# Fp32r products in one PSUM half: the 512-column head matmul becomes two matmuls of 256 columns

## What is computed

```python
proj = h @ w_in                      # even layer: SSD mixer and conformer convolution; odd layer: gated convolution and sparse attention
...
return jnp.concatenate([y, u], axis=-1) @ w_out

def conv_ffn(h, w_up, conv_w, conv_b, w_down):
    u = causal_dwconv(h @ w_up, conv_w, conv_b)
    g, v = jnp.split(u, 2, axis=-1)
    return (jax.nn.silu(g) * v) @ w_down
```

## Time and profile before

| | |
|---|---|
| device time, median of 3 runs | 2856.93 us (2853.34 to 2862.99) |
| profiled execution, span from first to last instruction | 2860.4 us |
| mean granted TensorE clock in it | 0.965 of 2.4 GHz |
| instructions | 41198 |

### The profile page before, as it was taken

One profiled execution on the slowest core, in us unless ns is written; L12 is line 12 of the kernel. 1 busy time (PEld: TensorE's weight loads), 2 busy tenths in 40 slices (PEclk: granted clock), 3 DMA queues, 4 the chain that ended last, 5 costly groups with the idle time before them and its releaser, 6 DMA issues.

```text
span 2860.4 us, 41198 instructions
## 1 busy us (share of the span) xinstructions
PE 2704.1 (95%) x15154; PEld 2330.6 (81%) x15154; DVE 1980.1 (69%) x2783; ACT 1328.3 (46%) x1716; POOL 418.8 (15%) x441
## 2 busy tenths in 40 slices
PE   6987788799999999999999999889999999999999
PEld 5866675688888888888888888767888888888887
DVE  6499987866776577567755576685667756675675
ACT  3444434344563455345433454463346634553553
POOL 4079953321000000000210000000210000000003
PEclk8888899899999999999989999999999999999999
DMA  5444441255555555555655566403555555555554
GB/s 177 134 145 132 132 132 60 78 186 185 184 190 183 184 190 183 185 191 172 190 158 164 176 178 190 132 1 100 187 184 187 180 190 188 180 190 187 182 177 145
DMA packets 238233, 464.26 MB, mean 162 GB/s; under 512 B 12474, under 2 KB 14138, under 8 KB 237882
## 3 DMA queue, kind: packets, MB, share of 16 engines
q1 hardware_dynamic: 234512, 459.96, 49.5%
q10 hardware_dynamic: 3626, 3.07, 0.4%
HBM read 460.90 MB, written 2.10 MB: 162 GB/s over the span
## 4 chain that ended last, share of the span: by engine, by line
PE 77%; DVE 14%; DMA 4%; ACT 2%; issue 1%; POOL 1%; SPq 0%; DVEq 0%; ACTq 0%; POOLq 0%
PE bank L1541 44%; PE bank L1540 22%; DVE weight_tail L954 4%; PE bank L1537 3%; DVE ca L1114 3%; DVE conv_acc L1095 2%; PE bank L1538 2%; ACT weight_head L572 1%; DMA weight_raw<-in_ffn_w_up 1%; PE bank L1725 1%; DMA w<-in_nsa_cmp_w 1%; DVE padded L963 1%; DMA weight_raw<-in_ffn_w_down 1%; PE bank L1802 0%; POOL stat L459 0%
## 5 line engine op out<-in xcount | busy, mean ns | idle before, releaser
L1541 PE MATMUL bank<-norm_in,weight_head 128*128 128x512 f32 x4440 | 1597.5, 402 | 0.0
L954 DVE TENSOR_TENSOR weight_tail<-weight_raw,weight_head 128x2048 fp32r<-128x2048 f32 (+1 forms) x456 | 1006.4, 2209 | 779.9 <-ACT weight_head L572 778.7
L572 ACT ACTIVATE weight_head<-weight_raw 128x2048 fp32r<-128x2048 f32 (+1 forms) x456 | 832.0, 1825 | 1049.7 <-DMA weight_raw<-in_ffn_w_up 330.6
L1540 PE MATMUL bank<-norm_in,weight_tail 128*128 128x256 f32 x4440 | 1258.0, 283 | 0.0
L1541 PEld LDWEIGHTS bank<-norm_in,weight_head 128*128 128x128 f32 x4440 | 844.2, 190 | 194.4
L1540 PEld LDWEIGHTS bank<-norm_in,weight_tail 128*128 128x128 f32 x4440 | 848.9, 191 | 13.5
L1541 PE MATMUL bank<-mixed,weight_head 128*128 128x512 f32 x2048 | 732.4, 400 | 0.0
L1540 PE MATMUL bank<-mixed,weight_tail 128*128 128x256 f32 x2048 | 577.9, 282 | 3.8 <-DVE mixed L1317 3.8
L1541 PEld LDWEIGHTS bank<-mixed,weight_head 128*128 128x128 f32 x2048 | 387.9, 189 | 89.1
L1540 PEld LDWEIGHTS bank<-mixed,weight_tail 128*128 128x128 f32 x2048 | 389.5, 190 | 9.9 <-DVE weight_tail L954 4.3
L453 POOL TENSOR_TENSOR squares<-residual 128x256 f32<-128x256 f32 x78 | 63.8, 818 | 2198.6 <-DVE residual L1256 2187.2
(11 more groups left out here) (264 smaller groups left out, 1751.4 us busy)
## 6 DMA issues: line engine op xcount, KB each, us to landing
weight_raw<-in_ffn_w_up SPq DMA_DIRECT2D x176, 1024.0 KB, 5.0
weight_raw<-in_ffn_w_down SPq DMA_DIRECT2D x64, 1024.0 KB, 5.0
weight_raw<-in_cd_w_in SPq DMA_DIRECT2D x64, 1024.0 KB, 5.7
weight_raw<-in_ab_w_in SPq DMA_DIRECT2D x56, 1024.0 KB, 5.1
weight_raw<-in_ab_w_out SPq DMA_DIRECT2D x32, 768.0 KB, 4.3
weight_raw<-in_ffn_w_down SPq DMA_DIRECT2D x32, 768.0 KB, 4.3
weight_raw<-in_cd_w_out SPq DMA_DIRECT2D x32, 768.0 KB, 4.3
x_stage<-in_x SPq DMA_DIRECT2D x2, 1024.0 KB, 6.4
```

What stands on the lines that cost most here:

```text
L572: act.activation(WHEAD[:, off % RING, 0:kt * CW], WRAW[:, off % RING, 0:kt * CW], ACT.Copy)\
L954: dve.tensor_tensor(WTAIL[:, off % RING, 0:kt * CW], WRAW[:, off % RING, 0:kt * CW], WHEAD[:, off % RING, 0:kt * CW].bitcast(F32), ALU.sub ...
L1540: pe.matmul(bank[c][:, 0:SEQ], tail, one, start=False, stop=False)
L1541: mm = pe.matmul(bank[c][:, :], head, both, start=False, stop=end)
```

## The change

Every pair becomes three matmuls of 256 columns that all add into columns 0 to 255 of the bank: tail times x head, head times x tail, head times x head. The second half of a bank is no longer used. ACT's copy and DVE's addition are gone: DVE multiplies the bank by `RSTD` directly into the target, or adds it once to the residual. The tables and semaphores that counted the copies are gone, and readers of `scaled` wait for `bank_read`, with the same count from the start of the span.

```diff
-            def copy_halves(e):
-
-                for c in range(4):
-                    act.wait_ge(cols_done, e * 4 + c - 3)
-                    act.activation(TMP[:, c, :], bank[c][:, SEQ:2 * SEQ], ACT.Copy).then_inc(half_copied, 1)
...
-            def read_banks(plain, tile, dst):
+            def read_banks(e, dst):
 
                 for c in range(4):
-                    dve.wait_ge(half_copied, plain + c + 1)
-                    dve.tensor_tensor(TMP[:, c, :], bank[c][:, 0:SEQ], TMP[:, c, :], ALU.add).then_inc(bank_read, 1)
-                    dve.wait_ge(bank_read, tile + c + 1)
-                    dve.tensor_tensor(dst(c), TMP[:, c, :], RSTD[:, :], ALU.mult).then_inc(scaled, 1)
+                    dve.wait_ge(cols_done, e * 4 + c - 3)
+                    dve.tensor_tensor(dst(c), bank[c][:, 0:SEQ], RSTD[:, :], ALU.mult).then_inc(bank_read, 1)
...
                     dve.wait_ge(cols_done, e * 4 + c - 3)
                     h = H[:, ds(i * 4 + c, 1), :]
-                    dve.tensor_tensor(h, bank[c][:, 0:SEQ].unsqueeze(1), h, ALU.add).then_inc(half_added, 1)
-                    dve.wait_ge(half_added, halves + c + 1)
-                    dve.tensor_tensor(h, bank[c][:, SEQ:2 * SEQ].unsqueeze(1), h, ALU.add).then_inc(bank_read, 1)
+                    dve.tensor_tensor(h, bank[c][:, 0:SEQ].unsqueeze(1), h, ALU.add).then_inc(bank_read, 1)
...
-                            both, one = rhs[:, u * s.kt + k, :], rhs[:, u * s.kt + k, 0:SEQ]
+                            xh, xt = rhs[:, u * s.kt + k, 0:SEQ], rhs[:, u * s.kt + k, SEQ:2 * SEQ]
                             begin, end = u == 0 and k == 0, u == s.units - 1 and k == s.kt - 1
-                            if begin:
-                                pe.matmul(bank[c][:, :], head, both, start=True, stop=False)
-                                mm = pe.matmul(bank[c][:, 0:SEQ], tail, one, start=False, stop=False)
-                            else:
-                                pe.matmul(bank[c][:, 0:SEQ], tail, one, start=False, stop=False)
-                                mm = pe.matmul(bank[c][:, :], head, both, start=False, stop=end)
+                            pe.matmul(bank[c][:, 0:SEQ], tail, xh, start=begin, stop=False)
+                            pe.matmul(bank[c][:, 0:SEQ], head, xt, start=False, stop=False)
+                            mm = pe.matmul(bank[c][:, 0:SEQ], head, xh, start=False, stop=end)
                         mm.then_inc(cols_done, 1)
```

More of the change, by code:

```diff
@@ L113, in rest @@
     return [kt_at(u) for u in range(e + 2, e + 6) if u < LAST_UNIT]
[L117 to L122, removed]
 EVEN_XBC_GROUPS = 6
@@ L133 @@
         _n += 2 * _c
[L136 to L141, removed]
 COMPRESS = (3, 5, 7)
@@ L616, in mlp @@
                     s, gate0 = SPANS[f"up{layer}{b}"], layer * FT + h0
-                    plain, conv = PLAIN[f"up{layer}{b}"], CONV[f"up{layer}{b}"]
+                    conv = CONV[f"up{layer}{b}"]
                     def turn(i, turns):
@@ L725, in _ @@
                 for c in range(4):
-                    done = PLAIN["in0"] + 4 * q + c + 1
+                    done = s.tile + 4 * q + c + 1
                     if 2 <= q < 4:
-                        act.wait_ge(scaled, done)
+                        act.wait_ge(bank_read, done)
                         act.activation(SG[:, c, :], YP[:, c, 3:3 + SEQ], ACT.Sigmoid).then_inc(glu_gate, 1)
@@ L863, in _ @@
                     for c in range(4):
-                        act.wait_ge(scaled, PLAIN["in1"] + 4 * q + c + 1)
+                        act.wait_ge(bank_read, s.tile + 4 * q + c + 1)
                         act.activation(SG[0:64, c, :], YP[64:128, c, 3:3 + SEQ], ACT.Copy).then_inc(swap_ready, 1)
@@ L1077, in _ @@
                 dst = data if q > 1 else lambda c: CA[:, 4 * q + c, :]
-                read_banks(PLAIN["in0"] + 4 * q, s.tile + 4 * q, dst)
+                read_banks(e, dst)
                 if last:
@@ L1246, in _, with residual_group @@
                 tails(e, k, kt_at(e + k))
-            def residual_group(t, halves, e, i, gain, uready, kts, norm=None):
+            def residual_group(e, i, gain, uready, kts, norm=None):
                 for c in range(4):
@@ L1274, in residual_groups @@
                 with dve.Fori(0, n) as i:
-                    residual_group(i * 4 + s.tile, i * 4 + HALVES[name], i * s.units + (s.unit + s.units), i, gain,
+                    residual_group(i * s.units + (s.unit + s.units), i, gain,
                                    i * 4 + uready, kts)
@@ L1296, in turn @@
                             e = i * 8 + first
-                            read_banks(i * 8 + (plain + 4 * half), i * 8 + (s.tile + 4 * half), data)
+                            read_banks(e, data)
                             tails(e, 2, kts[0])
@@ L1336, in mlp @@
                             e = s.unit + 4 * (i + 1)
-                            residual_group(s.tile + 4 * i, HALVES[name] + 4 * i, e, i, gain, 2 * DT + 4 * i, rest(e),
+                            residual_group(e, i, gain, 2 * DT + 4 * i, rest(e),
                                            3 if i == 3 and layer == 0 else None)
@@ L1382, in _ @@
                     dst = data
-                read_banks(PLAIN["in1"] + 4 * q, s.tile + 4 * q, dst)
+                read_banks(e, dst)
                 kts = ahead(e, 0, 1)
@@ L1399, in _ @@
                         j = 4 * (q - 12) + c
-                        dve.wait_ge(scaled, PLAIN["in1"] + 4 * q + c + 1)
+                        dve.wait_ge(bank_read, s.tile + 4 * q + c + 1)
                         dve.tensor_tensor(data(c), data(c), CA[:, j, :], ALU.mult).then_inc(conv_in, 1)
```

16 lines of the change are left out of this document (5 added, 11 removed).

## The result

The changed kernel takes 2895.24 us (median of four runs, 2892.97 to 2897.07) against 2855.25 us (four runs, 2853.34 to 2862.99): a ratio of 1.0133, interval 1.0118 to 1.0149. It is 40 us slower where 12 us less were forecast. The time lies inside the range, and within 3 us of rival 3, a small cost of its own for each matmul (2898). The profiled execution has a span of 2895.4 us at a mean granted clock of 0.967, against 2860.4 us at 0.965.

What follows compares the result with a forecast made beforehand. PE's stream of product matmuls was taken as the bound, except some 230 us in the first layer. Terms -10 + 1.1 - 1.8 - 1.2 = -12 us off the 2856.9 median gave 2845 us, range 2802 to 2905.

Steps and rivals of the forecast that it cites:

- rival 3: Product matmuls: each has a small cost of its own, up to 0.007 us, slot 0.12, +43 us, 2898; chance 0.20.
- Three slots of 256: Product matmuls on PE: three 256-column slots take 0.350 us against 0.353 a pair; -21 us, half taken, -10.
- Rival 4: Product matmuls: the excess belongs to instructions, 0.0167 us per load and matmul together, +107 us, 2963; chance 0.13.
- The stretch that PE does not bound: First layer, conformer sum: DVE's reads save 12.6 us, but the sum waits for POOL, ending near 400.1; +1.1 us.
- I leave the clock alone: First-layer stretch: PE idles some 13 us instead of 4.4, yet no clock effect is priced, at 0.87 there.
- The small terms: Bank reads: earlier release at four places after out or down, -1.8 us; three chain ends one link shorter, -1.2 us.
- Rival 5: First-layer stretch: POOL is not the bound, DVE's whole 12.6 us arrive, 14 us better, 2831; chance 0.08.
- Rival 2: Product matmuls: slots go towards the load's floor, 0.115 us or less, -54 us, 2802 or below; chance 0.09.

Runs made afterwards that it cites:

- experiment 1: Kernel before with its 512-column head matmul split into two of 256, except in a bank's first pair; copy and addition stay: 2895.37 us against 2859.03, ratio 1.0134.
- kernel 6: Changed kernel with POOL leaving out 14 of the 30 conformer taps of its last tile: 2870.62 us, one run.
- experiment 2: Changed kernel with every product matmul but the first of a bank cut to 128 columns: 4662.92 us, one run.
- kernel 7: Kernel before with POOL leaving out 14 of the 30 conformer taps of its last tile: 2860.07 us, one run.

## Why the prediction was wrong

**Three slots of 256 (-10 us): the step that failed.** It took the tail slot of before for the price of a 256-column matmul. Two faults lie in that. The first is rounding. "0.35 for three tails" is exact to 0.01 us, and the prediction priced that error at 21 us, where 0.01 x 6450 pairs is 64 us. That is just the way from its -21 to the +43 of three slots of 0.12. With the error at its true size the rows could not tell the sign, and a gain should not have been the forecast. The second is the kind of place: a slot in an alternating row holds the interplay of two sizes. The measured parts are these: the third matmul adds 13.3 ns, the alternation's 6 ns or so go, and 6 to 7 ns a pair remain. 6450 times that, +39 to +45 us, stands where -10 stood; shorter waits and the clock took a part of it back. The only place of the trace that showed two 256-column matmuls in a row, read 0.12 and 0.12. It was used to say "not longer by more than the rounding" where 0.120 against 0.1167 was the whole question. The windows held the answer's method, since a count of some 400 in 72 us is good to a quarter of a per cent. But no window of before held equal matmuls.

**Rival 3** was right in its mechanism and, by its upper value, in its price, but not in its parts: it took the fixed cost as 7 ns at most, where 13.3 were measured. Its slot of 0.12 came from reading. Its test in the window (600 against 615 matmuls) was met at 602. Rival 4 had the right owner, the instruction, and too high a price: it put the whole excess of the pair on two instructions, 16.7 ns each, where 13.3 are theirs.

The Trainium skill, TensorE: Matmul & The Clock Gate, section "Wait — 56ns, not 53.3ns?", has the right form, columns at 2.4 GHz and a fixed part for each matmul, and gives 2.5 ns for it. The `float32r` matmuls with their own load measured here pay 13.3 ns, five times as much.

**The stretch that PE does not bound (+1.1 us): right in kind, too small.** It measured +7.0, of which some 2.5 arise ahead of the stretch: POOL's and DVE's first conformer operations start 2.5 us later than before, and experiment 1, which keeps the old read, has 2.4 us too. Those belong to the third matmul. The read phase was forecast at 1.5 us and takes 1.40. DVE's conformer share was forecast to end near 386 us and ends at 387.03. DVE in the changed kernel:

```profile
364.56 22.55 DVE L1085 SCALAR_TENSOR_TENSOR ca<-conf_pad,params,ca 128x256 f32<-128x256 f32 x30
387.03 5.01 DVE L927 TENSOR_TENSOR weight_tail<-weight_raw,weight_head 128x2048 fp32r<-128x2048 f32 x2
391.96 1.40 DVE L934 TENSOR_TENSOR padded<-bank,rstd 128x256 f32<-128x256 f32 x4
393.28 4.68 DVE L927 TENSOR_TENSOR weight_tail<-weight_raw,weight_head 128x2048 fp32r<-128x2048 f32 x2
```

and POOL beside it:

```profile
386.92 0.77 POOL L465 TENSOR_TENSOR ca<-ca,squares 128x256 f32<-128x256 f32 x1
387.78 4.52 POOL L463 TENSOR_SCALAR squares<-conf_pad,params 128x256 f32<-128x256 f32 x1
...
393.21 2.61 POOL L463 TENSOR_SCALAR squares<-conf_pad,params 128x256 f32<-128x256 f32 x1
395.91 2.64 POOL L465 TENSOR_TENSOR ca<-ca,squares 128x256 f32<-128x256 f32 x1
...
405.52 0.40 POOL L466 COPY ca<-ca 128x256 f32<-128x256 f32 x1
```

Four tails met POOL, not two: the pair behind the next read was left out of the count. They cost it 4.52 - 0.53, 2.61 - 0.53 and 2.64 - 0.77, 7.9 us in all (0.53 us is the row of `L463` just before them) against 3.7 forecast. That is 4.2 us more than forecast, and with the 2.5 us by which POOL started later it covers the 5.8 us by which POOL ended later than forecast (405.9 against 400.1). The price for each tail, 2.0 us, was close to the 1.8 taken.

**"I leave the clock alone"**: nearly right here, wrong elsewhere. The sixteen matmuls of the sum have a median of 528 ns after the 21 us wait and 379 ns in kernel 6, where PE did not wait: some 2 us. But the kernel before has 634 ns there, after a wait of 4.4 us, so the longer wait made them no slower. In the attention the clock gave back 4.4 us and behind it about 3, which no term held. Why it was granted differently there is open.

**The small terms held.** Waits for the residual fell from 7.3 to 4.5 us (forecast -1.8 us), and the wait ahead of the attention from 1.02 to 0.61 us (forecast -0.4). The other two places of that term were not looked at. Rival 5, POOL as no bound, is excluded by experiment 6. Rival 2, a slot near the load's floor, did not occur with 256 columns; it did with 128 (experiment 2).

## What to carry to other kernels

Columns alone do not price a matmul. Splitting one into two costs a fixed part per instruction (here 13 ns), so a split must win it back on the engine that bounds the kernel, and relief on idle engines is worth nothing. Take a slot from a count over a long window in which only matmuls of that size run, or measure it so before the change; three timeline rows exact to 0.01 us can't carry a sum over 6450 repeats. Where two engines meet at one wait, relieve both: DVE's gain arrived only when POOL's share was cut as well. And price such a shift on both engines, since each slowed the other here.

## What the runs showed of the hardware

- At 2.4 GHz a `float32r` matmul of 256, 384 or 512 columns with its own load takes its columns and some 13 ns (13.0 to 13.5). Whether load or matmul holds that part was not separated.
- At the half clock no such part shows: 256 columns with a load take 0.213 us (the changed kernel from 1980.06 us), which is 256 columns at 1.2 GHz.
- With 128 columns the slot is not the columns'. It is 0.112 us at the full clock and 0.214 at the half one (kernel 2), and 60 columns take 0.111 too. That the 128x128 load sets it is my reading: it is what these matmuls share.
- The order of sizes has a price: 256 and 512 in turn take 0.353 us, in mirrored order 0.348, and by the equal rows they would take 0.346.
- The clock was at 0.50 through windows of 72 us in which PE was busy throughout, with matmuls of 128 columns (kernel 2). The profile's busy share and the granted clock are two different readings.
- A POOL operation that meets a `weight_tail` ends only when the tail does: 0.53 us become 4.52 beside two tails in a row (387.03 to 392.04). Beside DVE's conformer taps (`L1085`) POOL's addition takes 0.77 us, and 0.72 behind them. There it is DVE that pays: 30 taps take 21.2 us beside POOL and 12.0 with POOL idle (kernel 7). The Trainium skill, GPSIMD Engine Reference, section "Specifications", says that POOL's SBUF interfaces are shared with VectorE, and that POOL contends with DVE instructions in a 2-port perf mode or with two SBUF inputs. Tails and taps both have two such inputs, and both rows agree; which engine is slowed, and by how much, is in the rows alone.
